# Score groups of the hybrid attention step: the first two issued as one run with their masks behind them, and the third placed behind the last transposes in even steps

## The reference, cut to what matters

```python
ss = jnp.einsum('bqgrd,bgqnld->bgrqnl', qb, k_sel).reshape(Bn, G, R, Q_BLOCK, span)
p_sel = masked_softmax(ss, m_sel)...
o_sel = jnp.einsum('bgrqnl,bgqnld->bqgrd', p_sel.astype(dt), v_sel)
sw = jnp.einsum('bqgrd,bkgd->bgrqk', qb, kwb)
p_win = masked_softmax(sw, m_win)
o_win = jnp.einsum('bgrqk,bkgd->bqgrd', p_win.astype(dt), vwb)
...
o = gb[..., 0:1] * o_cmp + gb[..., 1:2] * o_sel + gb[..., 2:3] * o_win
```

## Time and profile before

| | |
|---|---|
| median of 3 runs | 3363.65 us (3362.55 to 3367.6) |
| the profiled execution | 3361.21 us, span 3359.5 us |
| PE, DVE, ACT busy | 99%, 59%, 41% of the span |
| granted PE clock, mean | 0.998 |
| attention loop of the first hybrid mixer | 2210.5 to 2286.7 us of the span |
| attention loop of the second | 2859.1 to 2935.2 us |

### The profile page before, as it was taken

The page is one execution under the profiler, slowest core; times in us unless marked ns, Lnnn a source line. Parts: engine busy times, 40 slices in busy tenths (PEclk is TensorE's granted clock), DMA queues, the critical chain, the costliest instruction groups (busy, mean ns, idle before and its releaser), DMA issues.

```text
span 3359.5 us, 44342 instructions
## 1 busy us (share of the span) xinstructions
PE 3318.8 (99%) x18719; PEld 2689.8 (80%) x18719; DVE 1981.7 (59%) x2904; ACT 1373.6 (41%) x2102; POOL 30.5 (1%) x68
## 2 busy tenths in 40 slices
PE   8999999999999999999999999999999999999998
PEld 7888878888888888886688888767888887588887
DVE  6554687675546653435564435586765465777644
ACT  4332367443324332326543323365543243654433
POOL 0000003000000000000000000000000000000000
PEclk9999999999999999999999999999999999999999
DMA  5444430244443432231123224211323242023221
GB/s 201 144 145 148 134 121 3 95 141 142 150 144 119 163 112 95 91 99 39 35 92 100 95 98 147 70 39 52 100 101 101 94 144 68 15 82 101 94 100 63
DMA packets 94230, 342.31 MB, mean 102 GB/s; under 512 B 10448, under 2 KB 13008, under 8 KB 93520
## 3 DMA queue, kind: packets, MB, share of 16 engines
q1 hardware_dynamic: 94032, 339.48, 30.6%
HBM read 337.34 MB, written 2.10 MB: 101 GB/s over the span
## 4 chain that ended last, share of the span: by engine, by line
PE 89%; DVE 6%; ACT 3%; issue 1%; POOL 0%; DMA 0%; SPq 0%; ACTq 0%; DVEq 0%; POOLq 0%
PE ps L818 21%; PE ps L819 21%; PE ps L820 21%; PE ps L923 2%; PE ps L924 2%; PE ps L927 2%; PE ps L972 1%; PE ps L974 1%; PE ps L973 1%; DVE SPL L2326 1%; PE ps L948 1%; PE ps L949 1%; PE ps L950 1%; DVE SML L3194 1%; ACT SPH L1613 1%; DVE WK L3210 1%
## 5 line engine op out<-in xcount | busy, mean ns | idle before, releaser
L2326 DVE TENSOR_TENSOR SPL<-RAW,SPH 128x1024 fp32r<-128x1024 f32 x522 | 635.4, 1223 | 872.3 <-ACT SPH L1613 871.9
L1613 ACT ACTIVATE SPH<-RAW 128x1024 fp32r<-128x1024 f32 x522 | 548.1, 1056 | 972.5 <-PE ps L820 869.8
L818 PE MATMUL ps<-HH,SPH 128*128 128x512 f32 x2312 | 909.9, 394 | 1.6 <-DVE SPL L2326 1.2
L820 PE MATMUL ps<-HH,SPL 128*128 128x512 f32 x2312 | 900.0, 389 | 0.0
L819 PE MATMUL ps<-HL,SPH 128*128 128x512 f32 x2312 | 900.0, 389 | 0.0
L818 PEld LDWEIGHTS ps<-HH,SPH 128*128 128x128 f32 x2312 | 434.0, 188 | 102.9 <-issue 10.8
L819 PEld LDWEIGHTS ps<-HL,SPH 128*128 128x128 f32 x2312 | 434.1, 188 | 92.3 <-issue 3.6
L820 PEld LDWEIGHTS ps<-HH,SPL 128*128 128x128 f32 x2312 | 434.0, 188 | 90.7
L818 PE MATMUL ps<-AH,SPH 128*128 128x512 f32 x996 | 389.0, 391 | 0.7 <-DVE AH L2678 0.7
L820 PE MATMUL ps<-AH,SPL 128*128 128x512 f32 x996 | 387.6, 389 | 0.0
L819 PE MATMUL ps<-AL,SPH 128*128 128x512 f32 x924 | 359.5, 389 | 0.0
(11 more groups left out here) (571 smaller groups left out, 4302.7 us busy)
## 6 DMA issues: line engine op xcount, KB each, us to landing
RAW<-in_ws SPq DMA_DIRECT2D x522, 512.0 KB, 3.3
RAW<-in_wa SPq DMA_DIRECT2D x96, 512.0 KB, 3.5
WK<-in_sm SPq DMA_DIRECT2D x2, 2784.0 KB, 10.1
WK<-in_cst SPq DMA_DIRECT2D x2, 1664.0 KB, 7.4
X<-in_x SPq DMA_DIRECT2D x8, 256.0 KB, 8.1
out<-X SPq DMA_DIRECT2D x16, 128.0 KB, 1.8
WK<-in_sm SPq DMA_DIRECT2D x1, 768.0 KB, 5.1
PCT<-in_pc SPq DMA_DIRECT2D x1, 349.0 KB, 3.1
```

The lines of the kernel that those rows point to most:

```text
L818: e.matmul(out, wh, rhs[0], start=start, stop=False)
L820: mm = e.matmul(out, wl, rhs[0], start=False, stop=stop)
L1613: e.activation(SPH[:, q:q + 1024], RAW[:, r:r + 1024], ACT.Copy).then_inc(hi_ready.did(("hi", n)))
L2326: e.tensor_tensor(SPL[:, q:q + 1024], RAW[:, r:r + 1024], SPH[:, q:q + 1024].bitcast(F32), ALU.subtract).then_inc(lo_ready.did(("lo", n)))
```

## The change

PE's `scores` takes several parts: it issues the fp32 matmuls of all of them and then their masks, part by part, each part with a signal of its own. Parts 0 and 1 of the next step go out in one such run, ahead of b0 (in step 0 behind b1). Part 2 stays behind b3 in odd steps and goes behind b4 in even ones. ACT's exponentials of part 2 move in the same way: behind the copy of b4 in even steps. DVE's order, the banks and what is computed are the same.

```diff
-                def scores(m, part):
+                def scores(m, *parts):
...
-                    masks = []
+                    masks = {part: [] for part in parts}
...
+                    for part in parts:
+                        for qt in ((3,), (2, 0), (1,))[part]:
+                            for g in range(2):
...
+                                masks[part].append(o[:, wd - 128:wd])
+                    for part in parts:
+                        for o in masks[part]:
+                            mm = e.matmul(o, H["IR"], H["CA"], start=False, stop=True, skip_group_check=True)
+                        mm.then_inc(pe_done.did(("qk", s, m, part)))
...
                     if 0 < m < 7:
-                        scores(m + 1, 0)
+                        scores(m + 1, 0, 1)
...
                         if i == 1 and m == 0:
-                            scores(1, 0)
-                        if i in (1, 3) and m < 7:
-                            scores(m + 1, (i + 1) // 2)
+                            scores(1, 0, 1)
+                        if i == (3 if m % 2 else 4) and m < 7:
+                            scores(m + 1, 2)
```

and in ACT's program:

```diff
-                        if i in (1, 3) and m < 7:
-                            scores(m + 1, (i + 1) // 2)
+                        if i == 1 and m < 7:
+                            scores(m + 1, 1)
+                        if i == (3 if m % 2 else 4) and m < 7:
+                            scores(m + 1, 2)
```

More of the change, by code:

```diff
@@ L1508, in hyb @@
                 qo, ko = [0, 128, 384, 768], [0, 512, 1024, 896]
-                def scores(m, part):
+                def scores(m, *parts):
                     r, kt_ = m // 2, (14, 15)[m % 2]
-                    masks = []
+                    masks = {part: [] for part in parts}
                     w.wait_ge(("caus", s), ("pj", s, QC[r]), ("pj", s, kt_))
[L1515 to L1525, removed]
+                    for part in parts:
+                        for qt in ((3,), (2, 0), (1,))[part]:
+                            for g in range(2):
+                                b, wd, p0 = ps["qk", s, m, part, g], 128 * (qt + 1), 64 * g
+                                w.wait_ge(*ps.before("qk", s, m, part, g))
+                                o = b[:, 128:512] if qt == 2 else b[:, 0:wd]
+                                e.matmul(o, wk(QC[r])[p0:p0 + 64, 128 * qt:128 * qt + 128], wk(kt_)[p0:p0 + 64, 0:wd],
+                                         start=qt != 0, stop=False, skip_group_check=True)
+                                masks[part].append(o[:, wd - 128:wd])
[3 more added lines that the diff above has]
+                        mm.then_inc(pe_done.did(("qk", s, m, part)))
                 def by_keys(m, i):
```

## The result

The changed kernel has a median of 3370.16 us in 17 runs, the kernel before 3362.97 in 17: +7.2 us, ratio 1.0019 with a 95% interval of 1.0013 to 1.0025. It is slower by more than the measurement's doubt, at the edge of the 0.2% that I had set. Forecast was +7.3 us.

The account below looks back on a forecast made before the run. The prediction took a chain from PE's b0 through ACT's queue to PE's last matmuls as the bound. Steps 0 to 6 summed to 3.6 us a loop, 7.3 for both: 3363.65 + 7.3 = 3371.0 us, range 3361 to 3377.

Parts of the forecast that it names:

- The chain: Both kinds of step: PE up to b0, then ACT's queue, then PE's last matmuls set the length; PE's other work has slack.
- The merged run: Parts 0 and 1 on PE ahead of b0: 2.27 us instead of 2.58, saving 0.31.
- The even step: Attention loop: 9.33 us against 9.02, about +0.3, with part 2 off the chain.
- The odd step: Attention loop: 11.17 us against 10.25, +0.92, with b0 on PE at 2.27 and its copy at 2.91.
- a term of 0.1 us: Odd step: late normalise puts the exponentials of part 0 at 3.50, where they could otherwise follow at 3.40.
- So moving part 2 earns most of the 1.09 back here: Even step: the 0.89 of part 2 leaves the chain, against b0 starting 1.09 later.
- b4's wait: Even step on PE: b4 waits some 1.3 us for the copy of b1 and holds part 2 behind it, at no cost.
- The rival that made it the culprit: b4's new wait makes normalise slide: half a microsecond in six steps, 6 us more, 3377 us; chance 0.15.
- The edges: Steps at the loop's ends: step 0 +0.2, step 1 +0.8 (11.1 us), step 6 +0.2, step 7 unchanged.
- PE setting the pace: Rival: PE rather than ACT ends the steps, so the change saves 11.8 us, 3352 us; chance 0.10.
- Edits that cancel: Rival: even steps give -0.6 each, -2.4 against +2.6 of the odd ones, near 3364 us; chance 0.17.
- the prediction's chain case: Main case, chance 0.58: spread 5.5 to 9.5 us slower, 0.36 of it above 0.2% (6.7 us), 0.22 below.

Follow-up runs that it names:

- masks apart: Changed kernel with the masks of parts 0 and 1 each behind its own part, both still ahead of b0: +9.2 us on the kernel before, ratio 1.0031.
- filler ahead: Changed kernel with 16 more mask matmuls a step at part 1, ahead of b0, about 0.9 us: +17.5 us on the kernel before, ratio 1.0052.
- filler at part 2: Changed kernel with 16 more mask matmuls a step at part 2, about 0.9 us: +12.9 us on the kernel before, ratio 1.0038.
- the merge alone: Changed kernel with part 2 behind b3 in every step, on PE and ACT: +11.2 us on the kernel before, ratio 1.0033.
- the move alone: Kernel before with only part 2 put behind b4 in even steps, on PE and ACT: +2.6 us, ratio 1.0007 (0.9998 to 1.0015).

## Why the prediction was right, and where its reasons were not

**The chain.** PE up to b0, ACT's queue, then PE's last matmuls: shown. 0.9 us ahead of b0 costs 0.7 to 0.8 in steps 1 to 5, the same work at part 2 costs 0.14 in steps 3 and 5. That PE is 99% busy says nothing of this. But this path is not alone: in both kinds of step the rows show a second one that ends 0.2 us or less from it, and the later of the two sets the step.

**The merged run.** 2.27 us forecast, 2.28 and 2.27 measured. The 0.31 that it saves is real on PE and worth 0.45 us a loop in the end, against masks apart.

**The even step.** 9.33 forecast, 9.35 measured, by the terms named: b0 at 2.27, copy of b2 at 7.24 (7.25: 2260.29 - 2253.04), copy of b4 right behind. Merge +0.86 and move -0.54 add up to the +0.33 found. The rows show a second path here: copy of b1, b4, part 2 and values back to back on PE. Worked out from the 0.20 left inside L1550 it ends at 9.15, and sums by it fit the runs: masks apart 9.15 + 0.31 = 9.46 (9.45 measured), filler ahead 9.15 + 0.90 = 10.05 (10.04), filler at part 2 the same (10.03). Step 6, which has no wait left inside L1550, is 9.15 long in the changed kernel and 9.45, 10.04 and 10.03 in these three.

**The odd step.** 11.17 forecast, 11.13 measured, and the rows follow the sum: exponentials of part 0 at 3.48 (forecast 3.50), copies of b1 and b2 at 4.82 (4.84), part 1 at 5.77 (5.81), copy of b4 at 8.46 (8.50), compressed values at 10.13 (10.17). The path was right, but the reason given beside it is half of it: "b0, and with it all of ACT's chain, starts 1.09 later". That alone does it: the merge alone gives 11.05. But the move alone gives 11.28, with no more work ahead of b0, and undoing the merge in odd steps leaves 11.28. There are two causes, each enough by itself, and they do not add. DVE's rows show the second, in step 3 of the kernel before and of the one after:

```profile
2238.22 2.46 DVE L3210 TENSOR_SCALAR WK<-WK,SML 128x128 f32<-128x128 f32 x8
2240.59 1.28 DVE L3194 TENSOR_REDUCE SML<-ps 128x1 f32<-128x512 f32 x2
```
```profile
2242.29 2.46 DVE L3214 TENSOR_SCALAR WK<-WK,SML 128x128 f32<-128x128 f32 x8
2244.66 1.28 DVE L3198 TENSOR_REDUCE SML<-ps 128x1 f32<-128x512 f32 x2
```

The first maxima follow normalise without idle time, 1.72 into the step before and 2.75 after: part 2's exponentials end the even step, normalise starts as the next one starts, and b0, b1 and the first maxima all wait for it. It was the later chain already before: in the earlier trace rows the exponentials of part 0 start 0.62 behind the copy of b0, in the earlier trace rows 0.49, so ACT's queue in the odd step had a small wait for DVE where the prediction saw no pause. After, normalise is still the later one, by 0.08 (3.48 against the 3.40 that b0 allows). The prediction had this as a term of 0.1 us and did not say that it would hold the step up by itself. With the later of two paths, 11.05 from b0 and 11.13 from normalise, other runs come out too: masks apart 11.05 + 0.31 = 11.36 (11.36), filler ahead 11.05 + 0.90 = 11.95 (11.94). The move alone is longer still, 11.28, because part 1 stands between b1 and b2 on PE and ACT's copy of b2 waits for it: the exponentials of part 1 start 1.11 behind the copy of b1, 0.95 with the merge. No run shortens normalise itself; its part is read from these rows and from the move.

**"So moving part 2 earns most of the 1.09 back here".** True beside the merge: it takes the loop from 81.80 to 79.86. By itself the same move lengthens the loop by 0.84. Which edit gets the blame hangs on the order in which they are counted: move first, +0.84 and then +2.81 for the merge; merge first, +5.59 and then -1.94 for the move. Merging in even steps is the part that costs most with everything else in place (8.48 to 9.35 in steps 2 and 4), and in step 0 it costs 0.74; in odd steps it then wins 0.14.

**b4's wait.** 1.3 us forecast and no cost: 1.17 us idle, no cost, shown by the kernel with part 2 ahead of b4 on PE. The rival that made it the culprit is out. The wait had only 0.2 us to spare, by the second path of the even step.

**The edges.** Step 0 0.2 longer (0.20: 8.22 against 8.03 from its part 0 on, and 0.01 ahead of it). That is the move's -0.54 and the merge's +0.74; the late first maxima were forecast to cost 0.84, and ACT's wait for them, before and after, grew by 0.86:

```profile
2213.61 0.69 ACT L2214 ACTIVATE WK<-ps,SML 128x512 f32<-128x512 f32 x1 [1.36 <-DVE SML L3194]
```
```profile
2216.18 0.69 ACT L2216 ACTIVATE WK<-ps,SML 128x512 f32<-128x512 f32 x1 [2.22 <-DVE SML L3198]
```

The others: step 1 came out at 11.13 (11.1 forecast), step 6 0.25 longer (0.2), step 7 unchanged at 9.4 from projection to projection.

**The rivals.** PE setting the pace is out by the merge alone and the two fillers. Edits that cancel are out by size: the move is not a gain of its own. The range, 3361 to 3377, was wide for a sum whose steps came out within 0.05 us each; its doubts lay in the mechanism, not in the durations. That "the same chain, summed from the rows, gives 9.02 and 10.25 exactly" was no support for it: the terms are read from start to start of the same rows, so they add up whatever the waits between them are due to. That the whole was met within 0.1 us is partly luck: the odd step came out 0.04 shorter than forecast, the even one 0.02 and step 6 0.05 longer. And whether a loss of this size would clear 0.2% was nearly even in the prediction's chain case (0.36 above, 0.22 below).

## What to carry to other kernels

Where three engines hand work round in a fixed order, lay their rows side by side for one period and write down the chain from step start to step start; the engine that is busiest by the page can be the one with the slack. An instruction run moved ahead of the one that another engine's in-order queue waits for can cost most of its length (here 0.80 and 0.86 of 1.09 us by itself), whatever it saves on its own engine, and little or nothing where a second path ends later anyway (odd steps beside the move). So write down the next-longest path as well. And test each half of a two-part edit alone: here two edits each make the odd step long by themselves, which neither the timeline after nor a correct sum tells.

## What the runs showed that was not expected

Two paths of an odd step lay 0.08 us apart, so that taking the merge out of odd steps changed them by only 0.14 us, and not downward. Between fp32 matmuls on half the rows and full-array masks the rows show about 0.2 us beyond the matmuls' own length (1.07 less 0.86), and the merge took one such change out as forecast (2.58 to 2.28); the rule of the Trainium skill's page "TensorEngine Tiling (Array Packing)", Key Properties, that a change of tiling mode drains the engine, agrees with that. No run here tells a drain from another cost at the same place.

Code that is the same in all kernels took between 2210.5 and 2213.6 us to reach the first loop in the profiles, a spread of 3.1 us, while the two loops of a kernel agreed within 0.04 us. Effects of a microsecond or two in 3363 were read from the loops for that reason.
